# A two-block model on one core: the first mixer's recurrence issued between projection tiles, and attention products issued one turn later

## The chip, the core and the metric

The kernel runs on one core of one Trainium2 chip. Its engines are TensorE (PE, with the weight loads PEld), VectorE (DVE), ScalarE (ACT), GpSimd (POOL) and SyncE (SP), each with its own instruction stream that it works off in order; semaphores join them. The metric is the device time of one execution in microseconds. A program of this size spreads some 0.1 to 0.2% from run to run.

## What is computed

256 tokens of width 1024 pass through two blocks, all in fp32. The first mixer is what the change is about:

```python
def hgrn2_chunked(q, k, logf, v, s0):
    bcum = jnp.cumsum(logf, axis=2)          # per chunk of 64 tokens
    blast = bcum[:, :, -1:]
    mid = 0.5 * blast
    q_in = q * jnp.exp(bcum - mid)
    k_in = k * jnp.exp(mid - bcum)
    scores = jnp.einsum('bnthd,bnshd->bnhts', q_in, k_in)
    ...
    o_intra = jnp.einsum('bnhts,bnshe->bnthe', scores, v)
    d_state = jnp.einsum('bnshd,bnshe->bnhde', k * jnp.exp(blast - bcum), v)
    ...
    o_inter = jnp.einsum('bnthd,bnhde->bnthe', q * jnp.exp(bcum), s_in)
```

It has 4 heads of width 128, a forward and a backward direction, and a starting state for each (`s0`) that comes from 256 context tokens: `s0 = sum over context of (k * exp(bcum_last - bcum))^T v`. Forget gates, keys and values are needed for context and tokens; q, an output gate `og`, the spatial gating inputs `u`, `v` and two merge gates `ga`, `gb` for the tokens only. The result is

```python
    o_a = rmsnorm(o_f + flip_seq(o_b), g_norm_a) * silu(og)
    o_b_mlp = chunk_sgu(gelu(u), gelu(v), ln_v_g, ln_v_b, w_s, b_s, n)   # layernorm of v, then W_s over 128 positions
    merged = sigmoid(ga) * (o_a @ w_pa) + sigmoid(gb) * (o_b_mlp @ w_pb)
    return merged @ w_o
```

A SwiGLU, a second block with gated linear attention, a retrieval over 16384 experts, a windowed attention of 16 heads with sinks, and a second retrieval follow.

## The kernel before

Activations lie with features on the partitions (`[P, k, T]`, T = 256 tokens, k = 8 blocks of 128), the first mixer's arrays in one arena (`M1`, L190). Weights come in panels of 1 MB through a ring of four slots: SP walks the list `SECTIONS` in order, and load n waits until panel n-4 has been used (L327). Panels of `w_in` (22 of 256 columns) alternate with panels of the modulation matrix `w_mod`. The latter aren't PE's: DVE multiplies and adds their eight blocks into `macc` (`mod_between` on DVE, L1241), and PE only turns the sum into columns with four small matmuls, one `w_in` panel later (`mod_between` on PE, L444). A panel's `proj` or `mod_acc` signal frees its slot.

The first six `w_in` panels are for context and tokens: four of forget logits (512 columns wide, two tiles each), two of values (four tiles each). The other 16 are for the tokens, two tiles a panel, each tile eight matmuls of 256 columns: q (tiles 0 to 3), og (4 to 7), u (8 to 11), v (12 to 15, by `proj_rows`), ga (16 to 23), gb (24 to 31). A tile goes into bank 4 or bank 5 in turn (`ring_bank`, L385), which must have been freed; ACT empties it with the function it needs (`evac`, L862). Transposes (`turn`, L494) take the same two banks.

The order of the first mixer, written out by hand on each engine:

- PE: all projection panels (L690 to L702); then for each direction and head a turn of the context weights and two products into bank 6, one at a time with DVE's copy (L707 to L718); then `lin` (L558): for a head `lin_pre` (turns of `kd`, scores, state products L522), one head ahead of `lin_out` (products with the masked scores L536, and with the states L553), then `ones` times the squares (L573); then the spatial mixing (L728), then w_pa, w_pb and w_o.
- In `lin_pre` the state products of direction 1 wait until DVE has made the three states of direction 0, since both use banks 6 and 7.
- ACT: sigmoids of the forget logits, values, both logs (L1047), the other evacuations, the root for the layer norm (L1064), then the exponentials of the context weights (L1070) and those of the recurrence (L1077 to L1081).
- DVE: modulation panels with the gates (L1564), both directions' "one minus f" (L1573) and scans (L1576, L1578), the other modulation panels, layer norm of v (L1592 to L1605), context weights (L1609), copies of the context states (L1614), exponents (L1622, L1623) and products (L1626 to L1629), then `lin`: masks (L1315), states (L1328), the norm with its reciprocal (L1339), and the gate (L1346).

The windowed attention runs head by head (L830 to L838): PE turns the probabilities of head h (L497), makes the scores of head h+2 (L816, L817), waits for ACT's copy of the turned probabilities, and makes the head's products (`att_out`, L826 to L828). DVE makes the max and, for the head before, the division (L1774 to L1791); ACT the exponentials (L1158) and copies.

## Time and profile before

| | us |
|---|---|
| median of 3 runs | 2939.48 |
| lowest and highest | 2933.36, 2940.86 |
| profiled execution | 2932.94 |
| its span in the trace | 2931.1 |
| PE busy | 2676.1 (91%) |
| DVE busy | 1692.2 (58%) |
| ACT busy | 1135.4 (39%) |
| mean granted clock of PE | 0.933 |

### The profile page before, as it was taken

How to read it: one execution, taken by the hardware profiler on the slowest of the kernel's cores; microseconds unless marked ns; L12 is line 12 of the kernel's file. 1: busy time of each engine (PE TensorE's matmuls, PEld its weight loads, DVE VectorE, ACT ScalarE, POOL GpSimd, SP SyncE). 2: the span in 40 equal slices, each digit the busy share in tenths (PEclk: the TensorE clock that was granted, in tenths of full speed). 3: DMA queues.
4: the chain of work that ended last, by engine and by line, in shares of the span. 5: the costliest groups of instructions: out<-in, count | busy, mean ns of one | idle time of the engine just before them, and what ended most of it. 6: DMA issues, size and time to landing. Idle time of an engine off the chain costs nothing.

```text
span 2931.1 us, 40829 instructions
## 1 busy us (share of the span) xinstructions
PE 2676.1 (91%) x15044; PEld 2308.5 (79%) x15044; DVE 1692.2 (58%) x3444; ACT 1135.4 (39%) x2327; POOL 3.5 (0%) x10
## 2 busy tenths in 40 slices
PE   8988489997877899999999996878999999999997
PEld 4677478854766799999988885746899999988886
DVE  3441534532644997778555557253698778655554
ACT  2111200002121155877455542222145877555553
POOL 0000000000000000000000000000000000000000
PEclk9998699998888899999999997857999999999998
DMA  6653036762643455444455556201245444455553
GB/s 240 221 203 115 0 115 244 272 231 73 247 155 115 166 181 187 140 137 143 159 197 189 196 191 227 99 23 58 101 163 183 144 145 144 147 198 187 199 188 113
DMA packets 65343, 471.55 MB, mean 161 GB/s; under 512 B 7297, under 2 KB 7553, under 8 KB 8241
## 3 DMA queue, kind: packets, MB, share of 16 engines
q1 hardware_dynamic: 64656, 467.85, 46.0%
q8 instruction: 98, 1.61, 0.2%
q10 hardware_dynamic: 272, 1.05, 0.1%
q0 software_dynamic: 272, 0.69, 0.1%
q14 instruction: 45, 0.36, 0.0%
HBM read 468.51 MB, written 1.05 MB: 160 GB/s over the span
## 4 chain that ended last, share of the span: by engine, by line
PE 83%; DVE 11%; issue 2%; DMA 2%; ACT 2%; SPq 0%; DVEq 0%; ACTq 0%
PE bank L621 25%; PE bank L667 24%; PE bank L481 18%; PE bank L633 4%; PE bank L491 3%; DVE macc L1256 3%; PE bank L752 2%; PE bank L465 2%; DMA ring<-in_w_up 1%; PE bank L497 1%; PE bank L406 1%; DVE macc L1227 1%; PE bank L553 1%; DVE arena L1372 0%; DVE nrm L1286 0%
## 5 line engine op out<-in xcount | busy, mean ns | idle before, releaser
L621 PE MATMUL bank<-h_split,t_split 128*128 128x256 f32 x6144 | 777.3, 286 | 13.6 <-DVE t_split L1454 13.6
L621 PEld LDWEIGHTS bank<-h_split,t_split 128*128 128x128 f32 x6144 | 751.5, 193 | 15.3 <-DVE t_split L1454 14.5
L1454 DVE TENSOR_TENSOR t_split<-ring,t_split 128x1024 fp32r<-128x1024 f32 x512 | 624.6, 1221 | 172.2 <-ACT t_split L931 170.8
L667 PE MATMUL bank<-t_split,w_split 128*128 128x512 f32 x3072 | 700.1, 390 | 3.6 <-ACT w_split L1004 3.6
L667 PEld LDWEIGHTS bank<-t_split,w_split 128*128 128x128 f32 x3072 | 578.7, 188 | 124.6 <-ACT t_split L1002 4.0
L481 PE MATMUL bank<-H,ring 128*128 128x256 f32 (+1 forms) x1728 | 422.3, 406 | 23.5 <-ACT H L880 11.9
L481 PEld LDWEIGHTS bank<-H,ring 128*128 128x128 f32 x1728 | 336.0, 196 | 100.1 <-issue 44.6
L1002 ACT ACTIVATE t_split<-ring 128x1024 fp32r<-128x1024 f32 x256 | 271.5, 1061 | 345.4 <-PE bank L667 252.6
L931 ACT ACTIVATE t_split<-ring 128x1024 fp32r<-128x1024 f32 x256 | 270.8, 1058 | 315.0 <-PE bank L621 282.6
L870 ACT ACTIVATE arena<-bank 128x256 f32<-128x256 f32 (+2 forms) x160 | 64.5, 405 | 566.2 <-PE bank L481 442.9
L1521 DVE TENSOR_TENSOR w_split<-arena,w_split 128x256 fp32r<-128x256 f32 x256 | 108.8, 425 | 298.1 <-ACT w_split L1004 298.1
L481 PE MATMUL bank<-arena,ring 128*128 128x256 f32 x1024 | 233.2, 390 | 24.1 <-DVE arena L1346 14.7
L481 PEld LDWEIGHTS bank<-arena,ring 128*128 128x128 f32 x1024 | 199.3, 196 | 54.0 <-DVE arena L1346 15.1
L1256 DVE SCALAR_TENSOR_TENSOR macc<-ring,cact,macc 128x256 f32<-128x256 f32 x448 | 217.2, 485 | 16.0
L1298 DVE SCALAR_TENSOR_TENSOR xT<-bank,modc,xT 128x256 f32<-128x256 f32 x48 | 22.4, 483 | 164.7 <-PE bank L481 83.5
L1004 ACT ACTIVATE w_split<-arena 128x256 fp32r (+1 forms) x256 | 102.4, 400 | 0.0
L497 PE MATMUL bank<-con,arena 128*128 128x128 f32 x136 | 37.2, 408 | 67.0 <-issue 24.0
L491 PE MATMUL bank<-ring,H 128*128 128x256 f32 x352 | 80.7, 390 | 4.2 <-DMA ring<-in_gla_v 4.2
L497 PEld LDWEIGHTS bank<-con,arena 128*128 128x128 f32 x136 | 21.8, 202 | 79.3 <-issue 25.1
L752 PE MATMUL bank<-ring,arena 128*128 128x512 f32 x176 | 79.7, 615 | 3.0 <-DMA ring<-in_w_down 3.0
L491 PEld LDWEIGHTS bank<-ring,H 128*128 128x128 f32 x352 | 68.5, 196 | 13.9 <-DMA ring<-in_gla_v 4.3
L944 ACT ACTIVATE arena<-bank 128x256 f32<-128x256 f32 (+32 forms) x230 | 72.5, 315 | 0.1
(254 smaller groups left out, 2110.9 us busy)
## 6 DMA issues: line engine op xcount, KB each, us to landing
ring<-in_peer_u SPq DMA_DIRECT2D x128, 1024.0 KB, 4.9
ring<-in_peer_v SPq DMA_DIRECT2D x128, 1024.0 KB, 4.9
ring<-in_mod_w SPq DMA_DIRECT2D x48, 1024.0 KB, 4.9
ring<-in_w_mod SPq DMA_DIRECT2D x24, 1024.0 KB, 4.9
ring<-in_w_in SPq DMA_DIRECT2D x22, 1024.0 KB, 5.0
ring<-in_w_up SPq DMA_DIRECT2D x22, 1024.0 KB, 5.2
ring<-in_peer_wq SPq DMA_DIRECT2D x16, 1024.0 KB, 4.9
ring<-in_w_down SPq DMA_DIRECT2D x11, 1024.0 KB, 4.9
```

Source lines behind the costliest of these rows:

```text
L481: last = mm(bank[:, 0:width], w[:, k, j * P:(j + 1) * P], rhs(k), start=(k == 0), stop=(k == ks - 1))
L491: last = mm(bank[:, 0:2 * P], lhs(k, tt), w[:, k, :], start=(k == 0), stop=(k == KT - 1))
L621: last = mm(bank[:, 0:T], u[:, a_, k, :], h_split[:, b_, k, :], start=(k == 0 and a_ + b_ == 0), stop=(k == KT - 1 and a_ == 1))
L633: last = mm(BK[6 + b][:, j * P:(j + 1) * P], P2[b][:, j, :], P1[b][:, j, :], start=True, stop=True)
L667: last = mm(BK[2 * tt + hf][:, :], w_split[:, j, a_, tt * P:(tt + 1) * P], t_split[:, j, b_, hf * 512:(hf + 1) * 512], start=(first and a_ ...
L752: last = mm(BK[2 * tt + x][:, :], hf[:, 2 * n + j, tt * P:(tt + 1) * P], w[:, j, x * 512:(x + 1) * 512], start=(n == 0 and j == 0), stop=( ...
L931: A(t_split[:, j, 0, :].rearrange("p (k c) -> p k c", k=KT), ring[:, r, :].rearrange("p (k j c) -> p j k c", k=KT, j=2)[:, j], ACT.Copy).t ...
L1002: A(t_split[:, j, 0, :].rearrange("p (k c) -> p k c", k=KT), ring[:, r, :].rearrange("p (j k c) -> p j k c", k=KT, j=2)[:, j], ACT.Copy).t ...
L1004: A(w_split[:, j, 0, :], arena[:, bass.ds(at * T, T)], ACT.Copy).then_inc(sems["w_hi"], 1)
L1256: ins = STT(acc, w[:, k, :], cact[:, c_col + k:c_col + k + 1], acc, MUL, ADD)
L1454: TT(t_split[:, j, 1, :].rearrange("p (k c) -> p k c", k=KT), ring[:, r, :].rearrange(view, k=KT, j=2)[:, j], t_split[:, j, 0, :].rearrang ...
L1521: TT(w_split[:, b % 2, 1, :], arena[:, bass.ds((i * 4 + b) * T, T)], w_split[:, b % 2, 0, :].bitcast(f32), SUB).then_inc(sems["w_ready"], 1)
```

## The change

- The context weights `W_` go to other arrays (St and oT), so that `qi` can be written earlier.
- PE: `lin_pre` is cut into turns, scores and states, and the first mixer no longer calls `lin`. The 32 token tiles are issued one at a time by `x_tiles`. Eight stand between a turn of the context weights and their products, four behind these, seven in the heads (one behind a head's scores, one ahead of its output products), one ahead of the squares and one behind the first head's scores, seven behind the squares and four behind the spatial mixing. The context products of a direction gather in bank 7 and are copied at once.
- ACT: the log and the exponentials of direction 0 stand among the forget tiles, those of direction 1 among the values; the evacuations of the tiles follow PE's order; the root for the layer norm comes behind the recurrence's own root.
- DVE: gates, scans and exponents of a direction stand between the modulation panels; "one minus f" comes behind the scans; the products with k come ahead of the last four modulation panels, those with q ahead of the last two; the layer norm of v comes behind `lin`.
- Attention: `att_out` of head h-1 stands behind the turn of head h and the scores of head h+2; on ACT, `att_copy(h-1)` stands behind the copy of head h.
- No load, no arithmetic and no byte moved is added or left out. The second block's `lin` keeps its order.

The core of the diff (PE, then attention, ACT, attention on ACT, DVE):

```diff
-        W_ = {0: M1["qi0"], 1: M1["qi1"]}
+        W_ = {0: M1["St"][:, 0:1024], 1: M1["oT"]}
...
+            def lin_states(m, h, dirs, E, vcols, behind):
+
                 for d in range(dirs):
-                    pe.wait_ge(*e.tile_out(dirs - d))
+                    pe.wait_ge(*e.tile_out(dirs - d + behind))
                     if e.refill("state"):
                         pe.wait_ge(sems["state"], e.freed("state"))
...
@@ -693,31 +705,69 @@
             for _ in range(2):
                 proj_rows(1, lambda k, tt: H[:, k, tt * P:(tt + 1) * P], 4)
                 mod_between(2)
-            for _ in range(4):
-                proj_cols(1, lambda k: Hx[:, k, :], T)
-                mod_between(1)
-            proj_cols(1, lambda k: Hx[:, k, :], T)
+            panel_now = [None, 0]
+
+            def x_tiles(n):
+
+                for _ in range(n):
+                    m = panel_now[1]
+                    if m % 2 == 0:
+                        panel_now[0] = next_panel().rearrange("p (k c) -> p k c", k=KT)
+                    w = panel_now[0]
+                    bank = ring_bank()
+                    for k in range(KT):
+                        half = slice(m % 2 * P, m % 2 * P + P)
+                        if m // 2 in (6, 7):
+                            last = mm(bank[:, 0:2 * P], Hx[:, k, half], w[:, k, :], start=(k == 0), stop=(k == KT - 1))
+                        else:
+                            last = mm(bank[:, 0:T], w[:, k, half], Hx[:, k, :], start=(k == 0), stop=(k == KT - 1))
+                    last.then_inc(sems["proj"], 1)
+                    panel_now[1] += 1
+
+            vN1 = M1["vN"].rearrange("p (t n) -> p t n", t=4)
+            kb = M1["kN"][:, 0:256].rearrange("p (t n) -> p t n", t=2)
+            for n in range(8):
+                d, h = n // 4, n % 4
+                if h == 0:
+                    pe.wait_ge(sems["wctx"], e.more("wctx"))
+                w = kt(W_[d], 4)
+                turn([w[:, h, 0:P], w[:, h, P:2 * P]])
+                x_tiles(1)
+                pe.wait_ge(*e.tile_out(2))
+                if n == 4:
+                    pe.wait_ge(sems["s0_in"], 1)
+                for tt in range(2):
+                    last = mm(BK[7][:, h * P:(h + 1) * P], kb[:, tt, :], vN1[:, tt, h * P:(h + 1) * P], start=(tt == 0), stop=(tt == 1))
+                if h == 3:
+                    last.then_inc(sems["s0"], 1)
+                if n % 2:
+                    mod_between(1)
+            x_tiles(1)
             mod_between(0)
-            proj_cols(1, lambda k: Hx[:, k, :], T)
-            proj_rows(2, lambda k, tt: Hx[:, k, tt * P:(tt + 1) * P], 2)
-            proj_cols(8, lambda k: Hx[:, k, :], T)
-
-            vN1 = M1["vN"].rearrange("p (t n) -> p t n", t=4)
-            for d in range(2):
-                pe.wait_ge(sems["wctx"], e.more("wctx"))
-                for h in range(HEADS):
-                    w = kt(W_[d], 4)
-                    turn([w[:, h, 0:P], w[:, h, P:2 * P]])
-                    pe.wait_ge(*e.tile_out())
-                    if e.refill("s0_in"):
-                        pe.wait_ge(sems["s0_in"], e.freed("s0_in"))
-                    kb = M1["kN"][:, 0:256].rearrange("p (t n) -> p t n", t=2)
-                    for tt in range(2):
-                        last = mm(BK[6][:, 0:P], kb[:, tt, :], vN1[:, tt, h * P:(h + 1) * P], start=(tt == 0), stop=(tt == 1))
-                    last.then_inc(sems["s0"], 1)
-            pe.wait_ge(sems["s0_in"], e.more("s0_in", 8))
+            x_tiles(3)
+
+            def v1(tt, h):
+                return vN1[:, 2 + tt, h * P:(h + 1) * P]
+
             S0 = M1["S0"].rearrange("p (d h n) -> p d h n", d=2, h=4)
-            lin(M1, 2, 1, lambda tt, h: vN1[:, 2 + tt, h * P:(h + 1) * P], lambda d, h: S0[:, d, h, :])
+            pe.wait_ge(sems["lin_in"], e.more("lin_in"))
+            lin_turns(M1, 0, 2)
+            lin_scores(M1, 0, 2)
+            x_tiles(1)
+            pe.wait_ge(sems["mod_bank"], 2)
+            pe.wait_ge(sems["s0_in"], 2)
+            lin_states(M1, 0, 2, 1, v1, 1)
+            for h in range(HEADS):
+                if h + 1 < HEADS:
+                    lin_turns(M1, h + 1, 2)
+                    lin_scores(M1, h + 1, 2)
+                    x_tiles(1)
+                    lin_states(M1, h + 1, 2, 1, v1, 1)
+                x_tiles(1)
+                lin_out(M1, h, 2, 1, v1, lambda d, h: S0[:, d, h, :])
+            x_tiles(1)
+            lin_squares(M1, 1)
+            x_tiles(7)
 
             pe.wait_ge(sems["vln"], e.more("vln", 1))
             pe.wait_ge(sems["mix_in"], e.more("mix_in", 48))
...
+            x_tiles(4)
             pe.wait_ge(sems["o_done"], e.more("o_done"))
             oT = kt(M1["oT"], 4)
             u4 = kt(M1["u"], 4)
...
                 turn([pS[:, h % 2, n * P:(n + 1) * P] for n in range(3)])
                 if h + 2 < 16:
                     att_scores(h + 2)
-                att_out(h)
+                if h:
+                    att_out(h - 1, 2)
+            att_out(15, 1)
             pe.wait_ge(sems["att_bank0"], e.more("att_bank0", 4))
             pe.wait_ge(sems["att_bank1"], e.more("att_bank1", 4))
             oS = kt(M4["oS"], 8)
...
+            forgets(0, range(4))
+            logs(0)
+            forgets(1, range(3))
+            ctx_weights(0)
+            inner_exps(0)
+            chunk_exps(0)
+            forgets(1, range(3, 4))
+            logs(1)
+            for tt in range(4):
+                values(0, tt)
+            values(1, 0)
+            ctx_weights(1)
+            inner_exps(1)
+            values(1, 1)
+            chunk_exps(1)
+            values(1, 2)
+            values(1, 3)
...
+            for n in range(8):
+                evac("turn", M1["kN"][:, 0:T], ACT.Copy)
+                x_tiles(1)
+            x_tiles(4)
+            lin_turned(M1, 0, 2)
+            x_tiles(1)
+            for h in range(HEADS):
+                if h + 1 < HEADS:
+                    lin_turned(M1, h + 1, 2)
+                    x_tiles(1)
+                x_tiles(1)
+                lin_copy(M1, h, 1)
+            x_tiles(1)
+            lin_root(M1["tB"])
+            x_tiles(5)
+            act.wait_ge(sems["vvar"], e.more("vvar"))
+            A(M1["stat"][:, 12:14], M1["stat"][:, 12:14], ACT.Sqrt).then_inc(sems["vstd"], 1)
+            x_tiles(2)
             e.tiles("turn", 4)
+            x_tiles(4)
...
                 evac("turn", pT[:, h % 2, :], ACT.Copy, width=3 * P)
-                act.wait_ge(sems["att_o"], e.more("att_o"))
-                if h % 2:
-                    j = h // 2
-                    A(kt(M4["oS"], 8)[:, j, :], BK[2 + j % 2][:, 0:T], ACT.Copy).then_inc(sems[f"att_bank{j % 2}"], 1)
+                if h:
+                    att_copy(h - 1)
+            att_copy(15)
...
+            used(1)
+            mod_between(2, 0)
+            used(1)
+            e.tiles("proj", 4)
+            gates(0)
+            mod_between(2, 0)
+            dve.wait_ge(sems["mix_in"], e.more("mix_in", 48))
+            scans(0)
+            exponents(0)
+            used(1)
+            mod_between(2, 0)
+            used(1)
+            e.tiles("proj", 4)
+            gates(1)
+            mod_between(2, 0)
+            scans(1)
+            exponents(1)
+            used(1)
+            mod_between(2, 0)
+            for d in range(2):
+                dve.wait_ge(sems["wexp"], e.more("wexp"))
+                TT(kt(W_[d], 4), kt(W_[d], 4), fg[d][:, :, 0:T], MUL).then_inc(sems["wctx"], 1)
+            used(1)
+            mod_between(2, 0)
+            dve.wait_ge(sems["exps"], e.more("exps"))
+            for d in range(2):
+                k4 = xpart(M1[f"fg{d}"])
+                TT(chunks(M1[f"ki{d}"]), chunks(M1[f"ki{d}"]), k4, MUL)
+                TT(chunks(M1[f"kd{d}"]), chunks(M1[f"kd{d}"]), k4, MUL)
+            used(1)
+            mod_between(1, 0)
+            used(1)
+            mod_between(1, 0)
...
+            e.tiles("proj", 8)
             for _ in range(4):
-                used(1)
-                mod_between(1, 0)
+                e.tiles("turn", 1)
+                e.tiles("proj", 1)
+            dve.wait_ge(*e.tile_out())
+            for d in range(2):
+                TT(M1[f"qi{d}"], M1[f"qi{d}"], M1["q"], MUL)
+                ins = TT(M1[f"qd{d}"], M1[f"qd{d}"], M1["q"], MUL)
+            ins.then_inc(sems["lin_in"], 1)
+            ctx_states(0)
+            used(1)
+            mod_between(1, 0)
+            used(1)
+            mod_between(1, 0)
             mod_out(16, 32, V("b_mod")[:, 16:48])
+            dve.memset(M1["sc"], 0.0).then_inc(sems["dve_step"], 1)
+            dve.wait_ge(sems["dve_step"], e.stepped())
+            ctx_states(1)
             used(2 + 2 + 8)
-            e.tiles("proj", 8 + 12 + 4)
-            dve.wait_ge(*e.tile_out())
-
+            for _ in range(4):
+                e.tiles("turn", 1)
+                e.tiles("proj", 1)
+            e.tiles("proj", 4 + 4)
+            e.tiles("turn", 6)
+            v_out = e.tile_out()
+            e.tiles("proj", 4 + 8)
+            e.tiles("turn", 2)
+            lin(M1, 2, 1, V("g_norm_a"), M1["tB"], P, lambda d, h: S0[:, d, h, :])
+
+            dve.wait_ge(*v_out)
             vS1 = M1["vS"].rearrange("p (t n) -> p t n", t=2)
```

## Rows read from the trace of the kernel before

**Rows 1.** The stage table: busy us (and instructions) of each engine in four stretches.

```profile
core 0: us, PE busy (x) PEld busy (x) DVE busy (x) ACT busy (x) POOL busy (x), PEclk, DMA share, GB/s
143.50:198.50 55.00, 47.12 (x219) 41.16 (x219) 33.64 (x59) 11.47 (x16) 0.00 (x0) 0.94 0.63 230
198.50:267.98 69.48, 69.05 (x320) 60.43 (x319) 1.93 (x5) 9.34 (x22) 0.00 (x0) 1.00 0.44 151
267.98:370.23 102.25, 48.95 (x297) 41.87 (x298) 49.97 (x90) 24.80 (x47) 0.00 (x0) 0.61 0.03 11
370.23:430.00 59.77, 57.77 (x261) 50.03 (x262) 15.17 (x36) 1.51 (x5) 0.00 (x0) 0.98 0.38 126
```

**Rows 2.** The chain of work: start us, us, what.

```profile
292.37 23.66 issue
...
370.23 28.85 PE bank L481 x128
```

**Rows 3.** PE by time, input projection: start, us, instructions, [idle before <-releaser].

```profile
114.11 14.06 PE L491 MATMUL bank<-ring,H 128*128 128x256 f32 x64
...
166.68 1.01 PE L451 MATMUL bank<-con,macc 128*128 128x1 f32 x4 [7.26 <-DVE macc L1256]
167.55 8.87 PE L481 MATMUL bank<-H,ring 128*128 128x256 f32 x32
...
212.13 55.42 PE L481 MATMUL bank<-H,ring 128*128 128x256 f32 x256
```

**Rows 4.** PE by time, context states and two heads of the recurrence.

```profile
290.81 1.22 PE L716 MATMUL bank<-arena 128*128 128x128 f32 x4 [0.47 <-ACT arena L870]
...
328.35 3.51 PE L553 MATMUL bank<-arena 128*128 128x64 f32 x16
...
336.95 1.16 PE L536 MATMUL bank<-arena 128*128 128x128 f32 x8
337.95 1.90 PE L553 MATMUL bank<-arena 128*128 128x64 f32 x16
339.68 0.61 PE L497 MATMUL bank<-con,arena 128*128 128x128 f32 x4
340.22 0.69 PE L510 MATMUL bank<-arena 128*64 128x64 f32 x16
...
343.48 0.68 PE L522 MATMUL bank<-arena 64*128 64x128 f32 x6 [1.90 <-DVE arena L1328]
```

**Rows 5.** DVE by time: a modulation panel, gates, scans, exponents, states, norm's reciprocal.

```profile
88.95 3.61 DVE L1256 SCALAR_TENSOR_TENSOR macc<-ring,cact,macc 128x256 f32<-128x256 f32 x7
92.48 1.91 DVE L1564 TENSOR_SCALAR arena<-arena,lbs 128x512 f32<-128x512 f32 x4
...
151.14 1.22 DVE L1573 TENSOR_SCALAR arena<-arena 128x2048 f32<-128x2048 f32 x1
152.28 4.56 DVE L1576 TENSOR_TENSOR_SCAN arena<-arena 128x512 f32<-128x512 f32 x4
...
293.47 1.43 DVE L1622 SCALAR_TENSOR_TENSOR arena<-arena 128x256 f32<-128x256 f32 x4
...
342.22 1.11 DVE L1328 SCALAR_TENSOR_TENSOR arena<-arena,bank 128x128 f32<-128x128 f32 x3
...
358.17 6.55 DVE L1339 RECIPROCAL arena<-arena 128x1024 f32<-128x1024 f32 x1 [1.12 <-ACT arena L909]
```

**Rows 6.** DMA issues of the stretch 50 to 300 us: count, size, us to landing.

```profile
ring<-in_w_in SPq DMA_DIRECT2D x21, 1024.0 KB, 4.9
```

**Rows 7.** ACT by time: a load of a function table and the activation behind it.

```profile
269.50 1.28 ACT L1070 ACT_TABLE_LOAD   x1
270.79 3.30 ACT L1070 ACTIVATE arena<-arena 128x256 f32<-128x256 f32 x8
```

**Rows 8.** The attention stage as a line of the stage table.

```profile
1925.80:2010.50 84.70, 63.31 (x209) 43.67 (x209) 38.43 (x144) 27.37 (x104) 0.00 (x0) 0.50 0.00 1
```

**Rows 9.** Attention by time: a head's turn, and DVE on the next scores.

```profile
1942.08 0.90 PE L497 MATMUL bank<-con,arena 128*128 128x128 f32 x3 [1.09 <-DVE arena L1791]
...
1944.60 0.56 DVE L1774 SCALAR_TENSOR_TENSOR arena<-bank,arena 128x384 f32<-128x384 f32 x1 [2.57 <-PE bank L817]
```

172 lines of the change are left out of this document (84 added, 88 removed).

## The prediction, made before the changed kernel ran

> **What bounds the kernel now.** I read the stage table first. PE works without a break in the input projection and in the output projections, at a granted clock of 1.00 and 0.98, but between them lies a stretch of 102.25 us in which it is busy 48.95 us at a mean clock of 0.61 [rows 1]. That stretch is the first mixer's recurrence, and nothing else runs in it: no DMA to speak of, DVE busy 50 us, ACT 25 us. The four engines wait for one another in a chain. The chain of work shows one wait of PE of 23.66 us in its midst, while DVE and ACT make exponents, and the next projection's start at 370.23 [rows 2]. The stretch ahead of it (143.5 to 198.5) has 7.9 us in which PE is idle [rows 1]; 7.26 of them are one wait, for a modulation panel that DVE sums only after its scans, and the first panel behind that wait takes 8.87 us where the 16 later tiles take 55.42 / 16 = 3.46 each, so 6.93 a panel [rows 3]. So what PE issues from 143.5 to 370.23 (226.7 us) is the matter of this change; behind 370.23 nothing changes but the attention.
>
> **Part 1, the recurrence between the tiles.** PE's work is the same set of instructions, now nearly in one piece, at the higher clock. I add it up from rows that lie in a stretch of full clock, or from half of those at the lower one:
> - 32 projection tiles of 3.46 [rows 3]: 110.7. Six modulation panels' turns, about 0.4 each (half of 1.01 for one at the low clock [rows 3]): 2.4.
> - Context states, eight times a turn and two products. 1.22 for the products at clock 0.50 [rows 4], so 0.61, and 0.3 for the two transposes (half of 0.61 for four): 8 x 0.91 = 7.3.
> - Per head: four transposes and the scores 0.61 + 0.69 less some 0.1 of overlap, 1.19, the states' products twice 0.6, the output 1.0 + 1.75 = 2.75 (1.16 and 1.90 less their overlap) [rows 4]. Four heads: 4 x 5.15 = 20.6. The squares, half a tile, 1.7. The spatial mixing, four groups of the shape of the states' products, 4 x 0.6 = 2.4.
>
> Sum 145.1 us. On top come waits that the interleaving doesn't take away:
> - Between a head's two directions the products of the second wait until DVE has made the three states of the first. In the row that wait is 1.90, of which DVE spent part on the masks [rows 4]; the masks are now made beside a tile, so the three state updates are left, 1.11 [rows 5], 1.3 with the semaphores. Nothing of the tile stands between the two directions, so it is paid four times: 5.2.
> - The ring. DVE's order is new: gates, scans and exponents of direction 0 now stand ahead of the modulation panels 12 and 13. A modulation panel costs DVE 3.9 (a first product, and seven more in 3.61 [rows 5]). From 84.7: gates 1.9, panels 10 and 11 7.8, scans 4.6, one minus f 1.2, exponents 1.4 + 1.2 [rows 5], panels 12 and 13 7.8: 110.8. The slot freed then takes the fifth w_in panel, which lands 4.9 later [rows 6], at 115.7; PE wants it at 114.1 [rows 3]: 1.6 late. By the same walk the sixth comes 0.6 late (DVE waits until 116.2 for the last forget tile, which now stands behind nine Exps on ACT, then gates, panels 14 and 15 until 126.0), and the seventh 1.2 late (scans, exponents, panels 16 and 17 until 142.2). Together 3.4, and the wait of 7.26 is gone, because by 165.6 DVE has panels 20 and 21 done.
> - The fifth context product waits for DVE to have copied the bank of the first four. DVE stands at four products with q, 1.2 each, that need the fourth q tile (by the walk PE ends it at 164.8 and it is evacuated at 165.2); then it copies, until 171, and PE is there at 169.5: 1.4.
> - Spatial mixing: two banks that DVE must empty, about 0.7.
>
> 10.7 us of waits. 143.5 + 145.1 + 10.7 = 299.3 against 370.23: 70.9 gained. The first output panels start on a warm PE: 28.85 now for 128 matmuls [rows 2], 27.7 by the rate of 256 in 55.42 [rows 3]: 1.1 more. So 72.0.
>
> What hides the rest, and by how much. The norm's chain (12 in all by the same steps of the old order, 6.55 of it the reciprocal [rows 5]) and then the layer norm of v (1.9, ACT's root, 4.2) run on DVE behind the squares, some 23.4 in all with the wait for the tile at which ACT turns to the root; seven tiles, 24.2, cover it with 0.8 to spare. Were the cover gone, it would cost what exceeds it, since four more tiles come only behind the mixing. Behind DVE's wait for the last modulation turn (about 189) are the cleared scores and the copy of the second context bank, which PE needs at 204. On ACT I count 14 changes of function table between 54 and 400 us instead of 8. A load takes 1.28 and the next activation starts 0.01 behind its end [rows 7]; the six more are 7.7 us on an engine with room, since each tile gives it 3.46 for an evacuation of 0.38, and none lies on PE's path.
>
> The Trainium skill ("ScalarE: Activation LUTs", What ACT_TABLE_LOAD costs) states a drain of about 1.4 us beside each load. The trace disagrees: no such gap stands between load and activation [rows 7]. By the page the layer norm's root would come 1.4 later, so 0.6 past its cover of 0.8, and the sum would be 71.4 instead of 72.0.
>
> What may be short in the sum is the clock. In the old stretch it falls during the output products of a head: 3.51 for 16 of them, against 1.90 in another head [rows 4]. Nothing in the trace shows recurrence and tiles mixed. The bounds: none of it (0), or each of the four outputs and the turn behind it at the low level (4 x 2.2 = 9). I take 3, nearer the lower end, because half the time is now dense tiles. Less than nothing is excluded, 1.00 being the top. So part 1 is **-69 us**.
>
> **Part 2, attention.** The products of a head move behind the next head's turn. The stage takes 84.70 us for 16 heads at clock 0.50 [rows 8], some 5.2 a head. The ring that sets this is: PE's turn and its scores of the head after next, 2.5 from the turn's start to that of DVE on these scores [rows 9]; then DVE's max and division, the other 2.7, and the next turn. The head's products, 1.6 (2.7 less the 1.09 that PE still waits for DVE [rows 9]), run while DVE works; they don't wait for ACT's copy, which is done by the time the scores are. So the move takes out a wait only for the last two heads, which have no scores behind the turn (0.6 each), and there it adds a head's products after the last turn (1.6): +0.4. I count 0, bounds -1.5 and +1.5.
>
> **Sum.** The profiled execution took 2932.94 (span 2931.1), the median of the runs is 2939.48. -69 gives a span of 2862, 2864 for such an execution and **2870.5** beside the median.
>
> **Rivals.**
> - The clock swings through the whole mixed stretch. The 60 us from the first head to the squares hold 54 us of work; with half of it at 1.2 GHz this costs 27 more than a sum without the clock term (2867.5), 2895. For it: the drop in the output products, and gaps of 1.3 in each head. Against: clock 1.00 where tiles run, 0.98 in the output projections, and 0.94 with a gap of 7.26 in the stretch [rows 1]. The Trainium skill ("TensorE: Matmul & The Clock Gate", A second HAM failure mode: psum-queue depth-cycling) says that short idle times between groups of matmuls can make the clock go up and down; the row at 8.87 us [rows 3] agrees as to a longer gap only. Chance 0.12.
> - The attention stage gets the higher clock, as its PE work is in one piece. PE's share of the ring, 2.4 us at 1.2 GHz, would halve: 16 x 1.2 = 19 less, 2851. Against: the pieces were contiguous before too. Chance 0.06.
> - It doesn't do what it says: the chain through DVE and ACT is longer than the tiles beside it, so PE waits at each joint (for the evacuated turns, for masks, for states) as now. With 2 us at each of the 17 joints of the context and head loops, half the gain goes: 2905. Against: DVE's steps for a head add up to 3.5 and a head has two tiles, 6.9. Chance 0.06.
> - Slower than before, by one mechanism: the shared two banks. A turn and a tile alternate on them, and ACT empties both in order; if ACT stood at a wait for each output sum or root, every tile of the mixed part would wait for it. The 20 tiles there would each have to pay over 3.5 us; ACT has about 1.5 us of work for a joint. Chance 0.03; at 5 us a tile it gives 2970.
>
> **How the numbers follow.** The forecast has 0.73. Its own range is 2861 to 2880: the clock term from 0 (2867.5) to 9 (2876.5), widened by the 6 us that the fastest run shown lies under the median and by 3 above. The range for 8 in 10 reaches some way into the two nearest rivals: 2855 to 2893. A measurement of this kernel tells 0.3% (9 us) from no change. Faster by more than that: all but the last rival and the extremes of the others, 0.95. Within: 0.02. Slower: 0.03.
>
> **What would show it.** In the changed kernel PE should be busy over 90% from 143 to 300 us at a clock near 1.00, the output projection should start near 300, loads of w_in panels should be waited for three times by about 1 us, and four waits of 1.3 for DVE's states should be there. The clock by stretches of 3 us in the heads tells the first rival, the window of the attention (84.7 us at 0.50) the second. The prediction is wrong if the layer norm is late, if ACT stands at table loads with full banks, or if the clock stays low past the first head.

## The result and the profile after

The changed kernel takes 2865.37 us (median of 4 runs, 2862.35 to 2868.17), the kernel before beside it 2936.42 (2932.78 to 2940.86). The ratio is 0.9749, 95% interval 0.973 to 0.9769. The prediction was 2870.5, range 2855 to 2893. The profiled execution took 2864.8 us with a span of 2863.0, against 2932.94 and 2931.1 before: 68.1 less, where the sum said 69. The agreement is closer than the steps behind it, as the sections below show, and it is in part luck: a second profile of each kernel shows 2927.2 and 2862.6, so 64.6 less.

The runs spread more than the 0.1 to 0.2% given ahead of the prediction. In 17 further runs the kernel before took 2935.17 to 2951.73 us, 0.6%, at a mean granted clock of 0.932 in the shortest and 0.927 in the longest. A difference of 5 us between two medians of four runs is therefore not a finding by itself.

The page of the changed kernel, PE's share and the granted clock in 40 slices (the clock's mean is 0.946, before 0.933):

```profile
PE 2658.2 (93%) x15044; PEld 2294.9 (80%) x15044; DVE 1691.4 (59%) x3438; ACT 1144.8 (40%) x2334; POOL 3.5 (0%) x10
...
PEclk9999999997989899999999996858999999999999
```

The stage table of the changed kernel; it answers [rows 1] and, in its last line, [rows 8]. The second and third lines are what the long recurrence has become:

```profile
core 0: us, PE busy (x) PEld busy (x) DVE busy (x) ACT busy (x) POOL busy (x), PEclk, DMA share, GB/s
143.50:198.50 55.00, 51.64 (x270) 45.55 (x269) 33.61 (x60) 10.11 (x22) 0.00 (x0) 0.97 0.65 238
198.50:262.00 63.50, 58.05 (x385) 49.84 (x384) 13.12 (x40) 10.09 (x28) 0.00 (x0) 0.97 0.25 86
262.00:304.50 42.50, 41.97 (x200) 36.70 (x199) 19.91 (x28) 10.48 (x17) 0.00 (x0) 1.00 0.35 124
...
1863.20:1946.40 83.20, 61.42 (x209) 42.91 (x209) 38.46 (x144) 27.50 (x104) 0.00 (x0) 0.51 0.00 1
```

The stretch of 102.25 us at a clock of 0.61 is gone. The heads lie in 63.5 us with PE busy 58.05 of them at 0.97, and the layer norm and spatial mixing in 42.5 us with PE busy 41.97 at 1.00. The attention stage is as it was, at 0.51.

The chain of work of the changed kernel, which answers [rows 2]. The "issue" of 23.66 us has no counterpart; the only DMA in the chain between 54 us and the output projection is one w_in panel:

```profile
109.37 5.99 DMA ring<-in_w_in
115.40 15.64 PE bank L491 x64
...
304.66 27.64 PE bank L481 x128
```

PE by time in the changed kernel, with the idle time before a row in brackets; it answers [rows 3] and [rows 4]. L491 and L723 are tiles of the projection (four and one to a row), L740 context products, L527 state products, L572 the squares, L778 the spatial mixing:

```profile
115.40 15.64 PE L491 MATMUL bank<-ring,H 128*128 128x256 f32 x64 [2.20 <-DMA ring<-in_w_in]
131.69 14.06 PE L491 MATMUL bank<-ring,H 128*128 128x256 f32 x64
147.04 3.72 PE L723 MATMUL bank<-H,ring 128*128 128x256 f32 x16 [0.23 <-DMA ring<-in_w_in]
...
171.77 0.68 PE L740 MATMUL bank<-arena 128*128 128x128 f32 x4 [3.13 <-DVE arena L1736]
172.50 5.31 PE L723 MATMUL bank<-H,ring 128*128 128x256 f32 x16
...
208.79 0.68 PE L527 MATMUL bank<-arena 64*128 64x128 f32 x6 [1.30 <-DVE arena L1438]
210.60 5.41 PE L721 MATMUL bank<-ring,H 128*128 128x256 f32 x16
...
261.66 1.89 PE L572 MATMUL bank<-arena,con 128*128 128x256 f32 x8
263.39 24.34 PE L723 MATMUL bank<-H,ring 128*128 128x256 f32 x112
287.56 1.84 PE L778 MATMUL bank<-small,arena 128*128 128x128 f32 x12
289.60 0.71 PE L778 MATMUL bank<-small,arena 128*128 128x128 f32 x4 [0.20 <-DVE macc L1791]
```

What to see: three kinds of wait (a load, 2.20 and 0.23; the copied context bank, 3.13; a head's states, 1.30, of which there are four) and, behind three of the waits, a group that takes longer than its equal: 15.64 where the next four tiles take 14.06, 5.31 where other tiles of that part take 3.62 to 3.72, 5.41 where the others take 3.72. Those three extras, 1.6, 1.7 and 1.7 us, are time at the lower clock. Behind 263.39 nothing waits: seven tiles in one piece, and the mixing finds its operands ready.

DVE by time in the changed kernel answers [rows 5]: the first of four products with q and the copy that PE waits for, ACT's root, and the last step of the layer norm.

```profile
166.40 1.22 DVE L1744 TENSOR_TENSOR arena<-arena 128x1024 f32<-128x1024 f32 x1
...
170.94 0.69 DVE L1736 COPY arena<-bank 128x512 f32<-128x512 f32 x1
...
282.78 0.17 DVE L1777 RECIPROCAL arena<-arena 128x2 f32<-128x2 f32 x1 [5.29 <-ACT arena L1185]
...
286.20 0.69 DVE L1784 TENSOR_TENSOR arena<-arena 128x512 f32<-128x512 f32 x1
```

The layer norm ends at 286.89 and PE comes to the mixing at 287.56: 0.67 us of cover were left. The row at 282.78 shows what fills the chain behind the squares: DVE stood idle for 5.29 us, because ACT takes the root only behind its evacuation of the fifth tile. A root further ahead in ACT's order might widen the cover; no run tries it.

The end of the attention in the changed kernel, PE by time, answers [rows 9]. A head's ring is unchanged (turns at 1930.95, 1936.10, 1941.25, so 5.15 apart, each behind a wait of 1.09 or 1.10). The last products now lie in one piece, the clock rises in them (0.63 becomes 0.39), and the projection starts warm:

```profile
1941.25 0.90 PE L497 MATMUL bank<-con,arena 128*128 128x128 f32 x3 [1.09 <-DVE arena L1945]
...
1944.30 0.60 PE L878 MATMUL bank<-arena 128*128 128x128 f32 x2
1944.72 0.39 PE L879 MATMUL bank<-arena 128*128 128x128 f32 x2
...
1946.37 27.86 PE L481 MATMUL bank<-arena,ring 128*128 128x256 f32 x128 [0.58 <-issue]
```

### The profile page after: what moved, and what is told of

It is laid out like the page before. It is cut to its first block, busy times and chain, and to the rows that moved or that the text cites. A ratio compares the mean times of both kernels' runs of the same rounds, so it can differ in the third digit from the quotient of the medians.

```text
span 2863.0 us, 40826 instructions
## 1 busy us (share of the span) xinstructions
PE 2658.2 (93%) x15044; PEld 2294.9 (80%) x15044; DVE 1691.4 (59%) x3438; ACT 1144.8 (40%) x2334; POOL 3.5 (0%) x10
## 4 chain that ended last, share of the span: by engine, by line
PE 83%; DVE 12%; DMA 2%; ACT 1%; issue 1%; SPq 0%; DVEq 0%
PE bank L633 25%; PE bank L679 24%; PE bank L481 14%; PE bank L645 4%; DVE macc L1366 3%; PE bank L723 3%; PE bank L803 2%; PE bank L491 2%; PE bank L465 2%; DMA ring<-in_w_up 1%; PE bank L406 1%; PE bank L497 1%; DVE macc L1337 1%; PE bank L721 1%; DVE arena L1482 0%
## 5 line engine op out<-in xcount | busy, mean ns | idle before, releaser
L481 PE MATMUL bank<-H,ring 128*128 128x256 f32 (+1 forms) x1280 | 323.4, 415 | 22.8 <-ACT H L933 11.9
L723 PE MATMUL bank<-H,ring 128*128 128x256 f32 x448 | 102.2, 386 | 0.5 <-DVE macc L1791 0.3
L723 PEld LDWEIGHTS bank<-H,ring 128*128 128x128 f32 x448 | 85.0, 193 | 12.7 <-DMA ring<-in_w_in 0.5
L491 PE MATMUL bank<-ring,H 128*128 128x256 f32 x288 | 68.1, 399 | 6.6 <-DMA ring<-in_gla_v 4.4
L803 PEld LDWEIGHTS bank<-ring,arena 128*128 128x128 f32 x176 | 33.8, 194 | 46.6 <-issue 42.4
```

Source lines behind the costliest of these rows:

```text
L481: last = mm(bank[:, 0:width], w[:, k, j * P:(j + 1) * P], rhs(k), start=(k == 0), stop=(k == ks - 1))
L491: last = mm(bank[:, 0:2 * P], lhs(k, tt), w[:, k, :], start=(k == 0), stop=(k == KT - 1))
L723: last = mm(bank[:, 0:T], w[:, k, half], Hx[:, k, :], start=(k == 0), stop=(k == KT - 1))
L803: last = mm(BK[2 * tt + x][:, :], hf[:, 2 * n + j, tt * P:(tt + 1) * P], w[:, j, x * 512:(x + 1) * 512], start=(n == 0 and j == 0), stop=( ...
```

## The experiments

In the comparisons inside the first mixer I count from the moment PE is ready for the fifth w_in panel (the start of that row less the wait before it) to the start of the output projection, since the whole front of a program moves by a microsecond or so from one profile to the next. In the changed kernel that is 304.50 - 113.20 = 191.3 us.

This stretch differs from profile to profile. The order of the first mixer is the same in four of them, and they show 191.3 (the changed kernel), 192.9 (its second profile), 191.7 (e7) and 194.4 (e1). The fifth panel is waited for 2.20, 2.60, 3.29 and 2.73 us, the context copy 3.13, 3.61, 3.60 and 3.60. So a difference of up to 3 us in this stretch can be the execution and not the edit. In the kernel before it is 255.9, 252.1 (its second profile) and 259.4 (e2): what differs there is the clock, for the output products of the four heads take 3.51, 1.90, 3.48 and 2.74 us in the first of these, 2.74, 1.90, 1.90 and 1.90 in the second and 3.51, 3.52, 3.52 and 2.34 in the third.

By total time, only e7 and e8 of the variants of the changed kernel stand clear of it. The intervals of the others' ratios overlap with one or both of its own two (0.973 to 0.9769, and 0.9742 to 0.9786), so what those edits do is read from the traces.

### Which half of the change does it: e1 and e2

e1 is the changed kernel with the attention in its old order (on PE, and ACT's copies alike):

```
-                if h:
-                    att_out(h - 1, 2)
-            att_out(15, 1)
+                att_out(h, 1)
```

> The changed kernel with the attention in its old order. Theory A (nearly all of the gain is the recurrence between the tiles; the attention's new order adds its last heads' waits and a warm start of the projection behind it, 3.3 us in the changed kernel's trace: 1.4 shorter stage, 1.9 shorter first 128 matmuls): 2868.5 against the median 2936.4 of before, ratio 0.977, and in the trace an attention stage of 84.6 us from its first scores to the projection, then 29.7 for 128 matmuls. Rival B (the attention stage owes its shorter end to chance of the clock, not to the order): the stage takes 83.2 here too and the time is 2865.

2873.53 us (2865.28 to 2876.95), ratio 0.9765 [0.9748, 0.9783]. The gain is the recurrence's. The attention stage takes 84.6 us here and the projection behind it 29.72, as expected; the 8 us above the changed kernel's median are more than the 3.3 expected, but 3.1 of them lie in the first mixer, where the two have one order.

e2 is the reverse, the kernel before with only the attention changed.

> The kernel before with only the attention products behind the next turn. Theory A: 3 us less than before, 2933, ratio 0.999; in the trace the stage takes 83.2 instead of 84.6 and the first 128 matmuls behind it 27.9 instead of 29.7; a head still takes 5.15 at clock 0.50. Rival B: no difference in either, 2936. Rival C (the order itself loosens the ring of a head): heads shorter than 5.15 and 10 us or more gained.

2936.9 us (2927.51 to 2945.76, 12 runs) beside 2940.62 of the kernel before; ratio 0.999 [0.9978, 1.0003], so no difference that can be told; of the expectation's two cases, 3 us less and none, the time decides neither. What happens locally is plain from the projection behind the attention, PE by time in e1 and then in e2:

```profile
1951.54 29.72 PE L481 MATMUL bank<-arena,ring 128*128 128x256 f32 x128 [0.52 <-issue]
```

```profile
2014.41 27.86 PE L481 MATMUL bank<-arena,ring 128*128 128x256 f32 x128 [0.58 <-issue]
...
2051.00 17.10 PE L481 MATMUL bank<-arena,ring 128*128 128x256 f32 x64 [3.98 <-ACT arena L882]
```

The last turn to the projection takes 5.1 us instead of 6.6 and the projection 1.9 less, but the first query panel behind it takes 17.10 where e1 has 15.46: half of the 3.3 us is given back by the clock within 40 us.

### The wait for the context copy: e3

The copy of the first four context products goes ahead of the four products with q:

```
+            ctx_states(0)
             dve.wait_ge(*e.tile_out())
...
-            ctx_states(0)
```

> The changed kernel with DVE's copy of the first context bank ahead of its four products with q instead of behind them. In the changed kernel PE waits 3.13 us for this copy and the tile behind takes 5.31 instead of 3.62 (the clock). Theory A (both are the price of that one place in DVE's order): the wait goes, the tile takes 3.6, the first output panel starts 4.8 us earlier relative to the panel at 115 us, and the time is 2861. Rival B (the clock's drop is owed to the small matmuls of the stretch, not to the wait): 3.1 us earlier only, the tile still takes over 5. Rival C: something behind it (loads, the last modulation panel) takes the place of the wait and nothing is gained.

2859.26 us (2855.38 to 2860.26), ratio 0.972 [0.9703, 0.9736]. PE by time in e3, a tile behind the fifth context product and the tile in the first head:

```profile
169.50 0.61 PE L740 MATMUL bank<-arena 128*128 128x128 f32 x4
170.16 3.70 PE L723 MATMUL bank<-H,ring 128*128 128x256 f32 x16
...
204.84 0.68 PE L527 MATMUL bank<-arena 64*128 64x128 f32 x6 [1.30 <-DVE arena L1438]
206.65 3.72 PE L721 MATMUL bank<-ring,H 128*128 128x256 f32 x16
```

The wait is gone, and the long tile behind it too. From the fifth panel to the output projection it takes 184.4 us, 6.9 less than in the changed kernel and 7.3 to 10.0 less than in the other three profiles of its order. What the edit surely takes away is the wait, 3.1 to 3.6 us, and what the clock costs behind it.

That price is not fixed. The tile behind the wait takes 5.31 in the changed kernel, 5.70 in its second profile, 5.97 in e1 and 4.32 in e7. In e6, whose order is the same up to there, the wait is as long and the tile takes no longer than others:

```profile
174.22 0.68 PE L740 MATMUL bank<-arena 128*128 128x128 f32 x4 [3.61 <-DVE arena L1735]
...
174.96 3.62 PE L723 MATMUL bank<-H,ring 128*128 128x256 f32 x16
```

The long tile of the heads is gone in e3 as well, but that can't be put down to the copy. It stands behind the first gap of 1.30 in the changed kernel (210.60) and in e1 (214.39), behind the second gap in the changed kernel's second profile (220.05), and it is absent in e6 and e7, which have the wait for the copy and the gaps of 1.30.

### The wait for the fifth panel: e4

```
             scans(0)
-            exponents(0)
             used(1)
             mod_between(2, 0)
+            exponents(0)
```

> The changed kernel with DVE's exponents of direction 0 behind the modulation panels 12 and 13 instead of ahead of them (2.6 us of DVE work that stands between a freed slot and the load of the fifth w_in panel). Theory A (the wait of 2.20 us for that load comes from DVE's new order): it goes, and with it the slow first part of that panel (15.64 instead of 14.06): 3.8 us less up to the sixth panel, time 2862. ACT's exponentials of direction 0 come about 1 us later, and the last forget tile is emptied about 1 us later, still in time. Rival B: ACT now stands longer at the exponents, the tile with the last forget logits blocks its bank, and PE waits for that instead: no gain or up to 2 us worse.

2863.46 us (2861.69 to 2871.27), ratio 0.9746 [0.9728, 0.9765]. PE by time in e4:

```profile
113.52 14.06 PE L491 MATMUL bank<-ring,H 128*128 128x256 f32 x64
...
130.52 14.08 PE L491 MATMUL bank<-ring,H 128*128 128x256 f32 x64 [2.15 <-DMA ring<-in_w_in]
...
148.26 5.41 PE L723 MATMUL bank<-H,ring 128*128 128x256 f32 x16 [2.60 <-DMA ring<-in_w_in]
```

The wait of 2.20 and its slow panel are gone, and waits of 2.15 and 2.60 stand ahead of the sixth and seventh, because DVE gets to the next gates only when ACT has the last forget tile (the gates start at 115.97, 115.05 in the changed kernel). The copy wait shrinks to 1.31. In all 188.7 us, 2.6 less than in the changed kernel, which is within what profiles of one order differ by. Removing one late load uncovered the next two.

### The waits inside a head: e5

```
-            x_tiles(1)
-            lin_states(M1, 0, 2, 1, v1, 1)
+            lin_states(M1, 0, 2, 1, v1, 0, 0)
+            x_tiles(1)
+            lin_states(M1, 0, 2, 1, v1, 1, 1)
```

The same in the loop over heads; the last argument is the direction.

> The changed kernel with each head's tile between its two directions' state products instead of ahead of both. Theory A (the wait of 1.30 us for DVE's three state updates, four times, is the one wait that the change left uncovered in the heads): it goes, 5.2 us less from the first head to the squares, and the clock's drop in the first head goes too or stays; 2860. Rival B: the products of direction 0 now stand right behind the scores and wait for ACT's copy of the turned keys, or DVE's masks come ahead of its states and the wait is only moved: 0 to 2 us less.

2864.04 us (2854.93 to 2871.32), ratio 0.9727 [0.9707, 0.9746]. PE by time in e5:

```profile
210.96 0.68 PE L527 MATMUL bank<-arena 64*128 64x128 f32 x6
211.57 3.72 PE L721 MATMUL bank<-ring,H 128*128 128x256 f32 x16
...
256.27 1.89 PE L572 MATMUL bank<-arena,con 128*128 128x256 f32 x8
```

All four waits of 1.30 are gone, and the long tile of the heads is too, though that one is also absent in e6 and e7, which keep the waits. From the first head's turns to the squares it is 53.2 us (from 203.04) instead of 60.15: 5.2 of waits, which are the edit's, and 1.7 of clock, which may be chance. The whole kernel shows less of it: 185.4 us in the mixer (5.9 less, as its copy wait is 3.60), and its second block is longer than that of the others, as told below. The profiled execution, 2871.32 us, is the longest of the four.

### The cover of the norms: e6 and e10

e6 puts five tiles instead of seven between squares and mixing, and the two behind the mixing.

> The changed kernel with five tiles instead of seven between the squares and the spatial mixing, the other two behind the mixing. It tests the cover of the norm's and layer norm's chain, put at 0.8 us of slack: in the changed kernel DVE ends the layer norm at 286.9 and PE comes at 287.6. Theory A (the slack is that small, and what is taken from the cover is paid): PE waits 6.2 us for the layer norm and takes the tiles behind at a lower clock, 1.6 more; 2873. Rival B (ACT or DVE get ahead when tiles move, so the chain is shorter than counted): under 3 us lost.

2871.78 us (2869.11 to 2874.86), ratio 0.9761 [0.9744, 0.9777], 6.4 above the changed kernel. PE by time in e6:

```profile
286.02 3.88 PE L778 MATMUL bank<-small,arena 128*128 128x128 f32 x16 [6.13 <-DVE arena L1783]
```

The wait is 6.13: two tiles, 6.92, less a slack of 0.8. This confirms the cover and its size. DVE stands idle for 5.29 us at ACT's root here too, which is again taken behind the fifth tile, now the last one.

e10 takes the eight tiles out of the heads and puts them behind the squares: the work of PE is the same, the recurrence stands alone again.

> The changed kernel with no tiles in the four heads: the eight that stood there come behind the squares. It asks what the tiles in the heads hide. Theory A (in the sum of the prediction the heads' own waits were 1.9 a head in the old order at full clock and are 1.3 with tiles; so tiles save only 0.6 to 1 us a head, and the clock): 2 to 4 us more for the waits and up to 6 for a clock that falls at the output products as in the kernel before; 2872. Rival B (the tiles in the heads are what the change lives by): 15 us more or above, 2880 to 2890.

2874.36 us (2870.24 to 2881.72), ratio 0.9774 [0.9753, 0.9794]; 200.3 us in the mixer, 9.0 more. PE by time in e10:

```profile
206.97 0.68 PE L527 MATMUL bank<-arena 64*128 64x128 f32 x6 [1.93 <-DVE arena L1433]
...
222.08 3.43 PE L558 MATMUL bank<-arena 128*128 128x64 f32 x16
...
232.98 3.51 PE L558 MATMUL bank<-arena 128*128 128x64 f32 x16
```

Without tiles the waits grow little (1.93, 1.42, 1.90 and 1.43, so 1.5 more in all). Most of the rest is the clock: the output products of the four heads take 2.26, 3.43, 3.51 and 2.44, near what they take in the old stretch [rows 4], against 1.90 with tiles around them. With tiles these products take 1.90 in every profile; without them one profile of the kernel before has 1.90 for three heads of four, and others for one or none. So the tiles in the heads do their work more by keeping the clock up than by filling waits; how much that is worth differs from one execution to the next.

### The attention's ring: e7

```
+                if h + 2 < 16:
+                    att_scores(h + 2)
                 pe.wait_ge(sems["att_p"], e.more("att_p"))
                 turn([pS[:, h % 2, n * P:(n + 1) * P] for n in range(3)])
-                if h + 2 < 16:
-                    att_scores(h + 2)
```

> The changed kernel with the attention's scores of head h+2 ahead of the wait for the probabilities of head h and its turn, instead of behind. It tests why moving the products did nothing for a head: by theory A the ring is turn, scores, DVE's max and division (2.5 + 2.7 us); with the scores ahead of the wait they leave the ring, and a head costs what PE has for it, 4.06 at clock 0.50, or about 2.8 if the clock then rises, where DVE's 2.6 is the bound: 17 to 38 us less, most likely about 30, 2835. Rival B (DVE's own chain or ACT's exponentials make the 5.15): no change. Rival C (the clock stays at 0.50 however dense PE is): 17 us less, 2848.

2843.44 us (2838.35 to 2851.31), ratio 0.9661 [0.9645, 0.9677]: 22 us under the changed kernel. PE by time in e7, one head:

```profile
1882.97 0.90 PE L497 MATMUL bank<-con,arena 128*128 128x128 f32 x3
1883.66 0.63 PE L877 MATMUL bank<-arena 128*128 128x128 f32 x2
...
1885.67 1.06 PE L868 MATMUL bank<-arena 64*128 64x256 f32 x2
1886.66 0.90 PE L497 MATMUL bank<-con,arena 128*128 128x128 f32 x3
```

The ring goes from 5.15 to 3.69 a head, the stage from 83.2 to 60.1 us. Between the second head and the last two PE waits no more and is now the bound itself, still at the lower clock: the same matmuls take the same 0.63 and 0.90. The higher clock that the expectation thought most likely (some 30 us) did not come; the result lies nearest its case of a low clock, 17 us. The ring named in the prediction (turn, scores of the head after next, DVE, next turn) was the right one; the change left it whole, and taking the scores out of it is what shortens the stage.

### The order of the front, and all together: e11 and e8

e11 has the order of e3, both exponents behind the modulation panels that follow them, and on ACT the last forget tile ahead of the chunk exponentials; the exponentials of direction 1 move behind later values likewise (not shown):

```
             inner_exps(0)
-            chunk_exps(0)
             forgets(1, range(3, 4))
             logs(1)
-            for tt in range(4):
+            values(0, 0)
+            chunk_exps(0)
+            for tt in range(1, 4):
                 values(0, tt)
```

> The changed kernel with the first context copy ahead of the q products (as in e3_copy_first), both directions' exponents behind the modulation panels that follow their scans, and on ACT the last forget tile and the second log ahead of the exponentials that aren't needed yet. e4_exponents_later removed the wait for the fifth w_in panel but PE then waited for the sixth and seventh, because the gates of direction 1 came no earlier. Theory A (the last forget tile's place on ACT sets the gates, these the modulation panels, and these the loads): the waits for the fifth to seventh panel and for the copy are all gone or under 0.5 us, no tile of the projection is slowed by the clock, and the first output panel starts about 10 us earlier, counted from the last forget tile (192.4 us in the changed kernel, 182 here): 2856. Rival B: values or turned weights now stand behind exponentials on ACT and block their bank; the waits only change their releaser, 186 or more.

2854.95 us (2850.51 to 2861.99), ratio 0.9721 [0.9695, 0.9747]. One load wait of 0.30 is left up to the heads, no group is longer than its equals, and the mixer takes 181.2 us: 10.1 less. The waits that e4 had uncovered are gone once the forget tile comes earlier on ACT. e11 changes several places at once, so that this one did it is likely but not shown alone.

e8 is e11 with e5's and e7's edits.

> Everything that helped together: the front order of e11_front_order, the tile between the two directions (e5_tile_between), and the attention's scores ahead of the turn (e7_scores_first). If the pieces are independent: 10 us, 5.2 us (the clock's share may be counted in both) and 22 us off the changed kernel's 2865: 2828 to 2830, ratio 0.963. Rival: with fewer gaps there is a new bound in the ring of loads (a panel in 5 us against 6.9 of PE), or the projection behind the attention starts at the low clock and gives back 2 us: 2833.

2824.85 us (2817.81 to 2831.35), ratio 0.9613 [0.959, 0.9637], 40 us faster than the changed kernel and 115 than the one before, somewhat more than the 2828 to 2830 expected. PE by time in e8 (the last row is cut by the window of the view; its start counts):

```profile
129.09 14.08 PE L491 MATMUL bank<-ring,H 128*128 128x256 f32 x64 [0.24 <-DMA ring<-in_w_in]
...
289.57 5.78 PE L481 MATMUL bank<-arena,ring 128*128 128x256 f32 x26
```

The mixer takes 175.6 us, 15.7 less; with the 23.1 of the attention that is 38.8 of the 40.

### Where equal work differs in time: both kernels again

> The changed kernel once more, beside e8_all and the kernel before on one chip, with its own profile. The ratio should be 0.975 to 0.977. The first profile has the second block's linear attention and its projection 3.7 us longer than the kernel before's, from the fourth gating panel to the first query panel, with the clock at 0.50 for longer. If that is the clock's chance from run to run, it is gone or different here; if it is a lasting cost of the change, it is here again, and it has been in all seven profiles of changed kernels.

> The kernel before once more, one look. In its first profile the second block's stretch from the fourth gating panel to the first query panel took 97.5 us; in the attention-only kernel, which has the same code up to there, it seems to have taken about 101. Chance from run to run: this profile shows 100 or 101. Otherwise 97.5 again.

The changed kernel again took 2867.19 us (2864.21 to 2874.82), ratio 0.9764 [0.9742, 0.9786]; the kernel before, in a single run, 2929.01. The question was the second block's linear attention, whose instructions neither half of the change touches. From its gating panel to the next query panel it takes 97.6 us in the kernel before, there again, and in e1; 101.2 or 101.3 in the changed kernel, there again, and in e2, e3, e4, e6, e10, e11 and e8; 105.1 in e5 and e7. PE by time in e1, where the gating panel starts at 772.07:

```profile
796.47 2.27 PE L558 MATMUL bank<-arena 128*128 128x64 f32 x12
798.90 0.45 PE L512 MATMUL bank<-arena 128*64 128x64 f32 x8
```

and in the changed kernel, where it starts at 765.07:

```profile
792.50 0.70 PE L512 MATMUL bank<-arena 128*64 128x64 f32 x8
...
797.46 1.64 PE L558 MATMUL bank<-arena 128*128 128x64 f32 x12
...
807.55 5.38 PE L572 MATMUL bank<-arena,con 128*128 128x256 f32 x16 [1.27 <-ACT arena L956]
```

The instructions are the same, and the waits too up to where the clock parts them; it rises in a row that starts 24.4 us into the stretch in the one and 32.4 in the other, where it also falls again in the squares (5.38; 3.69 in e1). At the program's end it is the other way round: a square sum of 16 matmuls takes 3.72 us in every program that has 101.2 or 101.3 above, and 6.27 or 6.31 in the kernel before, there again, and in e1, 6.25 in e5 and 5.87 in e7. In the kernel before and in the changed one the figures repeat, though the stretch starts 4 and 3 us apart in the two profiles of each.

So these differences go with the program and not with the execution. They came with the attention's change where that was made alone (e2), a thousand microseconds behind the stretch. But the attention's order does not decide them: e5 has the changed kernel's attention and differs only in the first mixer, and it has neither the 101.3 nor the 3.72. Nor do all changed kernels share a cost of 3.7, as the expectation had it: e1 has none, e5 and e7 twice that. Why the clock rises at another point in equal work was not settled: no run changed only where instructions lie.

## Why the prediction came out

**The bound and the mechanism held.** With e1 the recurrence's order alone gives nearly the whole gain, and the output projection starts at 304.50, where the working said 299.3 and with the clock 302.3. From the panel that PE was to begin at 114.1, that is 185.2 in the working and 191.3 measured: 6.1 more. By the terms:

- State updates between a head's directions: 4 x 1.30, predicted 5.2. Exact, and e5 removes exactly these.
- Loads of the fifth, sixth and seventh panel: 2.20, 0 and 0.23, predicted 1.6, 0.6 and 1.2. The walk through DVE's order came near (the slot came free at 109.37, predicted 110.8, but PE was ready 0.9 earlier and the load took 5.99 in the chain, not 4.9); the later two were absorbed because PE had lost time at the first, and in e4, where it had not, both are waited for. 1.0 less.
- Context copy: 3.13 instead of 1.4. PE was there at 168.64, 0.9 earlier than the walk had it, and DVE's copy ended at 171.6, not 171. 1.7 more.
- Spatial mixing: 0.20 and 0.30, predicted 0.7; a turn that ACT evacuates late, 0.26, was not in the sum.
- The clock: three extras of 1.6, 1.7 and 1.7, so 5.0 instead of 3, inside the bounds of 0 to 9. The other three profiles of this order have 6.0, 7.4 and 4.1 by the same count. I had put it at the heads' output products; with tiles around them these take 1.90 and cost nothing. It stands behind the two longest waits, and in three of the four profiles once in the heads.

These make 5.8 of the 6.1 (5.0 - 1.0 + 1.7 - 0.2 + 0.3). The terms that were mis-sized are the copy wait and the clock, and part of the second hangs on the first (e3).

**The cover.** Slack 0.67, predicted 0.8; e6 measured it a second way. The table loads of ACT, 14 between 54 us and the output projection as counted, showed nowhere on PE's path. One stands ahead of the layer norm's root (1.28 us, no gap on either side) and is part of the chain that the cover hides. The layer norm's root kept its cover, so the sum of 71.4 that the page of the Trainium skill ("ScalarE: Activation LUTs", What ACT_TABLE_LOAD costs) would have given by its drain did not arise.

**The warm start.** 28.85 became 27.64: 1.2, predicted 1.1.

**Attention.** The sum had 0 with bounds of 1.5 either way. In the profiles the stage is 1.4 shorter (84.62 to 83.18, first scores to projection), where the working had +0.4: for the last heads I had priced the added products at the lower clock, and they raised it. The projection behind is 1.9 shorter, 1.6 of which the next panel gives back. Net -1.7 in the profiles; e2 can't tell it from nothing.

**Why 69 nearly met 68.1.** Span by span: output projection 65.5 earlier (65.6 by the chain; predicted 67.9), 66.8 by the second output panel, 62.3 behind the second block's linear attention, 64.1 behind the attention; 63.4 in the last block's experts, then 1.6 and 3.0 more in the last experts and the program's end. So the front fell 2.4 short, attention's 1.7 made up most of that, and swings of 4.5 one way and 4.6 the other, which no step of the sum foresaw, nearly cancelled each other. In the second pair of profiles the output projection starts only 58.3 earlier (365.99 and 307.67) and the whole is 64.6; 3.8 of the 7.2 us between the pairs come from the old recurrence, in which the clock was up for longer in the second. The mechanism was right; that the sum came within 1 us of the first pair is luck. The range was needed: the swings are as large as most of the terms.

**The rivals.** That the clock swings through the whole mixed stretch is refuted by 0.97 in it. The Trainium skill ("TensorE: Matmul & The Clock Gate", A second HAM failure mode: psum-queue depth-cycling) warns of short idle times between groups of matmuls; here most gaps of 1.30 cost nothing (three of four in the changed kernel, all in e3, e4, e6, e7 and e11), while the gap of 2.20 was followed by a drop, and that of 3.13 too, though not its like of 3.61 in e6; so the trace agrees in part. That attention gets the higher clock is refuted by 0.51, and more sharply by e7, where PE has no gaps left and still shows the lower clock. That PE waits at each joint: of those that have a tile, only the one with the context copy does by more than 0.3. The shared banks never held a tile up.

## What to carry to other kernels

A wait of 2 to 4 us on a busy TensorE cost here its length and mostly 1 to 3 us more, through the lower clock in the group behind it; so remove it, if only by the order of the engine that is late, here one copy moved ahead of four products. When independent tiles are put between the steps of a chain, give each joint a tile, also the one between the two directions of a head, and check which later steps live on the cover that is left (here 0.67 us). An order changed outside the ring that sets a stage's time does next to nothing: attention needed the next scores ahead of the wait, and the stage gained 23 us from that and 1.4 from the rest. Before you put a few microseconds of one trace down to an edit, profile the same kernel again: one order of the mixer showed 191.3 to 194.4 here.

## What the runs showed of the hardware

- Waits of 2.20 to 3.29 us for the fifth panel were followed by a group of 15.60 to 16.97 us instead of 14.06, in all eight profiles that have them. Waits of 3.13 to 3.61 for the context copy were followed by a tile of 5.30 to 5.97 us instead of 3.62 in five profiles, of 4.32 in e7 and of 3.62 in e6. In e4 a gap of 2.15 was not followed by a slower group, and one of 2.60 seventeen microseconds later was (5.41).
- The old recurrence, alone between long gaps, is not at one clock: the same 16 output products of a head took from 1.90 to 3.52 us, and three profiles of the old first mixer, from the fifth panel on, came out at 252.1, 255.9 and 259.4 us.
- The attention of e7, in which groups of short matmuls keep PE busy for 56.31 of 60.9 us, stayed at a clock of 0.52: leaving out the gaps didn't raise it.
- In the second block's linear attention the same instructions saw the clock rise in a row 24.4 or 32.4 us into the stretch, alike in both profiles of the kernel before and in both of the changed one, which is worth 3.7 us.
- A load of 1 MB took 4.9 us by the median between 50 and 300 us; the one that PE waits for took 5.99 in the changed kernel.
